# A transformer layer's first projection: the first two token tiles in halves by turns, smaller early loads, and one fold moved ahead

## The reference, cut to what matters

```
h = rmsnorm(x, p['norm_mix_g'])
z = h @ p['w_in']                    # x: tokens x 1024, w_in: 1024 x 2576
gq, gk, gv, gr, ga, pu, dq, dk, dv = jnp.split(z, idx, axis=-1)
```

## Time and profile before

| | us |
|---|---|
| median of 3 runs | 747.88 (747.49 to 748.06) |
| profiled execution, its own time | 748.39 |
| its span | 746.5 |
| PE busy in it | 684.6 (92%) |
| DVE, ACT, POOL busy | 521.9, 424.1, 142.3 |

### The profile page before, as it was taken

The page is one execution under the profiler, slowest core; times in us unless marked ns, Lnnn a source line. Parts: engine busy times, 40 slices in busy tenths (PEclk is TensorE's granted clock), DMA queues, the critical chain, the costliest instruction groups (busy, mean ns, idle before and its releaser), DMA issues.

```text
span 746.5 us, 9430 instructions
## 1 busy us (share of the span) xinstructions
PE 684.6 (92%) x3469; PEld 550.8 (74%) x3469; DVE 521.9 (70%) x697; ACT 424.1 (57%) x602; POOL 142.3 (19%) x160
## 2 busy tenths in 40 slices
PE   4999999998887998889999589999999999999992
PEld 3898887776655675668888568888888888878861
DVE  4436745565577656266456779888999999988883
ACT  5635642245453443163334528888888788777881
POOL 4102840011000101100000220222222222222134
PEclk9999999999899999899999669999999999999997
DMA  8623242303771000130045879999999999999863
GB/s 305 211 82 152 94 159 99 113 22 114 261 283 69 2 1 0 57 141 0 1 177 219 293 278 326 369 389 366 384 379 375 382 374 375 373 369 382 321 215 128
DMA packets 32867, 161.23 MB, mean 216 GB/s; under 512 B 6189, under 2 KB 6523, under 8 KB 18108
## 3 DMA queue, kind: packets, MB, share of 16 engines
q1 hardware_dynamic: 23392, 140.39, 49.6%
q0 software_dynamic: 5344, 10.27, 5.1%
q10 hardware_dynamic: 4092, 10.08, 3.7%
HBM read 149.59 MB, written 20.03 MB: 227 GB/s over the span
## 4 chain that ended last, share of the span: by engine, by line
PE 71%; DVE 16%; DMA 4%; ACT 4%; issue 3%; POOL 1%; SPq 1%; POOLq 0%; DVEq 0%; ACTq 0%
PE pj L2111 41%; PE scores L2111 13%; PE tr_v L2111 10%; DVE wl L1414 4%; PE tr_a L2119 2%; PE scores L2491 2%; PE tr_v L2119 2%; DMA acc_rows<-y,idx_sb 1%; DMA xs_next<-acc_rows,idx_sb 1%; DVE w_lo L1414 1%; PE tr_a L2520 1%; ACT prob L1133 1%; DMA xT_raw<-in_xT 1%; DVE tiny L1667 1%; DVE w_lo L1443 1%
## 5 line engine op out<-in xcount | busy, mean ns | idle before, releaser
L1414 DVE TENSOR_TENSOR wl<-moe_raw,wh 128x2048 fp32r<-128x2048 f32 x96 | 218.5, 2290 | 26.9 <-ACT wh L901 26.1
L901 ACT ACTIVATE wh<-moe_raw 128x2048 fp32r<-128x2048 f32 x96 | 182.3, 1919 | 37.7 <-PE scores L2111 12.3
L2111 PE MATMUL pj<-w_hi,xT_hi 128*128 128x512 f32 (+2 forms) x192 | 70.9, 369 | 9.5 <-DVE w_lo L1443 7.8
L747 POOL TENSOR_SCALAR rs<-stat 128x1 f32<-128x1 f32 (+4 forms) x31 | 11.1, 359 | 338.1 <-ACT sq_scr L913 181.0
L2111 PE MATMUL pj<-w_hi,xT_lo 128*128 128x512 f32 (+2 forms) x192 | 69.1, 360 | 0.0
L2111 PE MATMUL pj<-w_lo,xT_hi 128*128 128x512 f32 (+2 forms) x192 | 69.1, 360 | 0.0
L802 POOL DMA_INDIRECT acc_rows<-y,idx_sb x14 | 22.3, 1590 | 206.3 <-ACT y L1337 192.2
L2111 PE MATMUL pj<-wh,xgh 128*128 128x512 f32 x128 | 52.2, 408 | 1.4 <-DVE xgl L1414 1.4
L1443 DVE SCALAR_TENSOR_TENSOR w_lo<-raw,pack_a,w_hi 128x512 fp32r<-128x512 f32 (+2 forms) x64 | 43.8, 744 | 12.2 <-ACT w_hi L945 12.1
L2111 PE MATMUL tr_v<-wh,xgh 128*128 128x512 f32 x128 | 51.1, 399 | 0.0
L2111 PE MATMUL pj<-wh,xgl 128*128 128x512 f32 x128 | 50.5, 395 | 0.0
(11 more groups left out here) (416 smaller groups left out, 1500.6 us busy)
## 6 DMA issues: line engine op xcount, KB each, us to landing
moe_raw<-in_w_exp_gate SPq DMA_DIRECT2D x32, 1024.0 KB, 8.9
moe_raw<-in_w_exp_up SPq DMA_DIRECT2D x32, 1024.0 KB, 10.2
moe_raw<-in_w_exp_down SPq DMA_DIRECT2D x32, 1024.0 KB, 10.7
raw<-in_dense SPq DMA_DIRECT2D x16, 1024.0 KB, 5.9
raw<-in_dense SPq DMA_DIRECT2D x8, 256.0 KB, 6.9
x_rows<-in_x_prompt SPq DMA_DIRECT2D x4, 512.0 KB, 11.0
xw<-in_x_prompt ACTq DMA_DIRECT2D x1, 2048.0 KB, 8.5
h_rows<-h ACTq DMA_DIRECT2D x4, 512.0 KB, 3.6
```

Source lines behind the costliest of these rows:

```text
L747: link(pool.tensor_scalar(rs[rows, n, cs], stat[rows, n, cs], EPS, None, ALU.add))
L901: act.activation(wh[s4][:, :], moe_raw[n % RING][:, :], ACT.Copy).then_inc(hi_done, 1)
L1414: return dve.tensor_tensor(out, a, b, op)
L2111: return pe.matmul(out, lhsT, rhs, start=start, stop=stop, skip_group_check=True)
```

## The change

**Loads.** x tiles 0, 1 and 2 are loaded in halves (x_half), the first half of tile 1 ahead of the last quarter of unit 0; the second half of tile 1, both halves of tile 2 and tile 3 follow unit 1, and only then rows 0, rows 1, x tile 4, rows 2, unit 2, and so on. ACT's first load takes only 27 columns of pack_a; the other 316 are loaded by ACT after the high part of x tile 4, and DVE waits for them (pack_in) ahead of their first use.

**Products.** PE takes G tiles 0 and 1 half by half in turn: k 0 to 3 of tile 0, k 0 to 3 of tile 1, k 4 to 7 of tile 0, k 4 to 7 of tile 1. Tile 2 is taken in two halves as well. G tiles 2 and 3 go to the last two banks of `scores`, G tiles 0, 1 and 4 to pj0, pj1, pj0. The transposes come one tile later (tile t-3 ahead of tile t for t = 3, 4; tile 2 ahead of R tile 0; tiles 3 and 4 after R tiles 0 and 1).

**ACT and DVE.** High and low parts follow the new order of arrival; all of x tiles 1 to 3 stand ahead of squares 0 and 1. The split of unit 2 stands ahead of the copy of G tile 2 as before, that of unit 3 after it. On DVE the fold of the sample tile of G stands ahead of the copies of tile 3's transpose, where it stood ahead of tile 4's.

```diff
-    plan = [((b, t), row_reader(t)) for b, _, _ in IN_BLOCKS[:-1] for t in range(TILES)] + [(("Q", t), "A") for t in range(2)]
+    plan = [(("G", t), row_reader(t), (0, 1, 2, 3, 0)[t]) for t in range(TILES)]
+    plan += [((b, t), row_reader(t)) for b, _, _ in IN_BLOCKS[1:-1] for t in range(TILES)] + [(("Q", t), "A") for t in range(2)]
     for t in range(TILES):
...
         sc = ctx.enter_context(nc.psum_tensor("scores", [P, 4 * 512], F32))
+        pj_more = [sc[:, 1024:1536], sc[:, 1536:2048]]
+        pj_of = lambda key: (pj + pj_more)[PJ[key][3]]
...
         moe_in = [sem(f"moe_in{i}") for i in range(RING)]
-        x_in, x0_in = [sem(f"x_in{t}") for t in range(TILES)], [sem(f"x0_in{g}") for g in range(2)]
+        x_in, xh_in = {t: sem(f"x_in{t}") for t in (3, 4)}, [[sem(f"x{t}_in{g}") for g in range(2)] for t in range(3)]
         part_in = [[sem(f"unit{n}_in{k}") for k in range(4)] for n in range(2)]
...
         x_again = sem("x_again")
-        gains_in = sem("gains_in")
+        gains_in, pack_in = sem("gains_in"), sem("pack_in")
         mem_in, params_in, hist_in, state_in = sem("mem_in"), sem("params_in"), sem("hist_in"), sem("state_in")
...
-            for n in range(2):
-                ks = slice(4 * n, 4 * n + 4)
-                sp.dma_start(xT_raw[:, 0, ks, :], A["xT"][0][:, ks, :]).then_inc(x0_in[n], 16)
+            def x_half(t, g):
+                ks = slice(4 * g, 4 * g + 4)
+                sp.dma_start(xT_raw[:, t, ks, :], A["xT"][t][:, ks, :]).then_inc(xh_in[t][g], 16)
+
+            def quarter(n, k):
+                c = slice(512 * k, 512 * k + 512)
+                sp.dma_start(raw[:, n, c], unit(n)[:, c]).then_inc(part_in[n][k], 16)
+
+            for g in range(2):
+                x_half(0, g)
                 for k in range(4):
-                    c = slice(512 * k, 512 * k + 512)
-                    sp.dma_start(raw[:, n, c], unit(n)[:, c]).then_inc(part_in[n][k], 16)
-            for t in range(1, 4):
-                x_load(t)
-                rows_load(t - 1)
+                    quarter(g, k)
+                    if (g, k) == (0, 2):
+                        x_half(1, 0)
+            x_half(1, 1)
+            x_half(2, 0)
+            x_half(2, 1)
+            x_load(3)
+            rows_load(0)
+            rows_load(1)
+            x_load(4)
+            rows_load(2)
             dense_load(2)
-            x_load(4)
             rows_load(3)
...
-            act.dma_start(pack_a[:, :], A["pack_a"]).then_inc(gains_in, 16)
+            act.dma_start(pack_a[:, 0:27], A["pack_a"][:, 0:27]).then_inc(gains_in, 16)
...
-            def x0_high(g):
+            def x_half_high(t, g):
                 ks = slice(4 * g, 4 * g + 4)
-                act.wait_ge(x0_in[g], 16)
-                act.activation(xT_hi[:, 0, ks, :], xT_raw[:, 0, ks, :], ACT.Copy).then_inc(xT_hi_done, 1)
+                act.wait_ge(xh_in[t][g], 16)
+                act.activation(xT_hi[:, t, ks, :], xT_raw[:, t, ks, :], ACT.Copy).then_inc(xT_hi_done, 1)
...
-            x0_high(0)
+            x_half_high(0, 0)
             act.wait_ge(gains_in, 16)
             w_high(0)
-            x0_high(1)
+            x_half_high(1, 0)
+            x_half_high(0, 1)
             w_high(1)
+            x_half_high(1, 1)
+            for g in range(2):
+                x_half_high(2, g)
+            x_high(3)
             act.wait_ge(consts, 1)
             for t in range(2):
-                x_high(t + 1)
                 x_square(t)
+            x_high(4)
+            act.dma_start(pack_a[:, 27:], A["pack_a"][:, 27:]).then_inc(pack_in, 16)
             act.dma_start(pack_b[:, :], A["pack_b"]).then_inc(params_in, 16)
...
             for t in range(4):
-                if t >= 2:
-                    w_high(t)
+                if t == 2:
+                    w_high(2)
                 n = t
...
                 pj_out(("G", t), rowbuf[0:r, n % 2, 0:256], rs[0:r, 1, t:t + 1],
-                       pj[PJ[("G", t)][3]][0:r, 0:256]).then_inc(act_step, 1)
+                       pj_of(("G", t))[0:r, 0:256]).then_inc(act_step, 1)
                 steps[0] += 1
                 pj_out(("G", t), gv[0:r, t, :], rs[0:r, 1, t:t + 1],
-                       pj[PJ[("G", t)][3]][0:r, 256:512]).then_inc(pj_act, 1)
-                if t < 2:
-                    x_high(t + 3)
+                       pj_of(("G", t))[0:r, 256:512]).then_inc(pj_act, 1)
+                if t == 2:
+                    w_high(3)
                 if t < 3:
...
-            def x0_low(g):
+            def x_half_low(t, g, n):
                 ks = slice(4 * g, 4 * g + 4)
-                dve.wait_ge(xT_hi_done, g + 1)
-                tt(xT_lo[:, 0, ks, :], xT_raw[:, 0, ks, :], xT_hi[:, 0, ks, :].bitcast(F32), ALU.subtract).then_inc(xT_lo_done, 1)
+                dve.wait_ge(xT_hi_done, n)
+                tt(xT_lo[:, t, ks, :], xT_raw[:, t, ks, :], xT_hi[:, t, ks, :].bitcast(F32), ALU.subtract).then_inc(xT_lo_done, 1)
             def x_low(t):
-                dve.wait_ge(xT_hi_done, t + 2)
+                dve.wait_ge(xT_hi_done, t + 4)
                 if t < 4:
...
             link(dve.memset(lg[:, :, :], 0.0))
-            for n in range(2):
-                x0_low(n)
-                w_low(n)
-            for t in range(1, TILES):
-                x_low(t)
+            x_half_low(0, 0, 1)
+            w_low(0)
+            x_half_low(1, 0, 2)
+            x_half_low(0, 1, 3)
+            w_low(1)
+            x_half_low(1, 1, 4)
+            for g in range(2):
+                x_half_low(2, g, 5 + g)
+            x_low(3)
+            x_low(4)
...
             for t in range(TILES):
-                if t in (2, 3):
-                    w_low(t)
-                if t == 4:
+                if t in (1, 2):
+                    w_low(t + 1)
+                if t == 3:
                     n = ROW_AT[("G", 4)]
...
             dve.tensor_reduce(lams[:, 1:2], lamv[:, 2, :], AX.X, ALU.add).then_inc(lam_sum, 1)
+            dve.wait_ge(pack_in, 16)
             link(dve.tensor_scalar(gdiff[:, :], gdiff[:, :], 1.0 - LAM_INIT, None, ALU.mult))
...
                     claim("pj", PJ, PJ_KEYS, key, pj_act, pj_dve)
-                out = pj[j][:, 0:w]
+                out = pj_of(key)[:, 0:w]
                 for k in range(nk) if part is None else range(part * nk // 2, (part + 1) * nk // 2):
                     n, c = units[k // 4], slice(w * (k % 4), w * (k % 4) + w)
-                    if key == ("G", 0) and k == 4:
-                        pe.wait_ge(xT_lo_done, 2)
                     if t == 0:
...
                 for t in range(TILES):
-                    pe.wait_ge(xT_lo_done, t + 2 if t else 1)
                     project((b, t), t, *x_block(t), BLOCK_UNITS[b], WIDTH[b])
...
-            in_block("G", 2, {})
-            in_block("R", 0, {0: lambda: rows_T("G", 4, 2)})
+            for part in range(2):
+                for t in range(2):
+                    pe.wait_ge(xT_lo_done, 2 * part + t + 1)
+                    project(("G", t), t, *x_block(t), BLOCK_UNITS["G"], WIDTH["G"], part)
+            for part in range(2):
+                pe.wait_ge(xT_lo_done, 5 + part)
+                project(("G", 2), 2, *x_block(2), BLOCK_UNITS["G"], WIDTH["G"], part)
+            for t in range(3, TILES):
+                rows_T("G", t - 3, 2)
+                pe.wait_ge(xT_lo_done, t + 4)
+                project(("G", t), t, *x_block(t), BLOCK_UNITS["G"], WIDTH["G"])
+            rows_T("G", 2, 2)
+            in_block("R", 0, {0: lambda: rows_T("G", 3, 2), 1: lambda: rows_T("G", 4, 2)})
             in_block("U", 2, {0: gate_T, 1: gate_logits})
...
```

## The result

The first comparison gave 740.87 us median (739.99 to 742.88, 4 runs) against 747.88 (747.49 to 748.06), a ratio of 0.9907 [0.9888, 0.9927]: 7.0 us less, below the forecast range. It did not hold at that size. The same two kernels compared twice more gave 743.39 against 746.55, 0.9949 [0.9922, 0.9976], and 743.18 against 747.96, 0.9941 [0.9914, 0.9967]. Over all executions that are listed with their mean granted clock (the share of 2.4 GHz that the matmul clock had over the execution), the kernel before has a mean of 746.92 us (133 runs, 742.05 to 752.61, standard error 0.20) and the changed one 742.73 (26 runs, 739.83 to 746.83, error 0.43). So the change takes off **4.2 us (error 0.5)**, 0.56%, or 3.9 without the four executions of the first comparison; the forecast was 2.2.

What follows compares the result with a forecast made beforehand. PE, busy 92% of the span, was taken as the bound, with time to win where it waits or runs slowly. Gains of 1.96 and 0.3 us, rounded to 2.2, took 747.88 to 745.7, range 744.6 to 747.5.

Steps and rivals of the forecast that it cites:

- The hole: Block G, between tiles 0 and 1: PE waits for x tile 1, 2.08 us from start to start; predicted to go.
- 36.3 (2.2 before 38.5): Sign in the trace after: block R's first matmul near 36.3 us, 2.2 us sooner than before.
- the sum of 2.26: Whole forecast gain, 1.96 us from the turns plus 0.3 from the smaller first load, rounded to 2.2.
- Together 1.96: Turns in block G: 1.85 us of waiting for x tile 1 and 0.11 of a slow first step saved.
- I take 0.3: Smaller first load of pack_a, at PE's start and unit 0's fourth quarter: 0.3 us gain, from 0 to 0.5.
- the rise of the clock I let move with PE's start: Block G: the step from 1.2 to 2.4 GHz, 4.8 us after PE's first matmul, assumed to shift with that matmul.
- the runs' scatter of 0.3: Whole-kernel time: run-to-run scatter of 0.3 us, used in setting the range's lower end at 744.6.
- Rival 1: Clock rises later in block G (1.8 us lost, 747.5) or has another half low stretch at 188-200 us (1.7); chance 0.17.
- The parts priced at nothing: G tiles 2 and 3 in `scores` banks, later transposes, and the moved fold: each priced at 0 us.
- hold PE about 2 us: Ahead of R tile 1: the fold behind the copy of tile 3's transpose would end 2.5 us later, delaying PE.
- Rival 2: Gains come late: pack_a's small piece takes 5.8 us instead of 3.6, delaying unit 0's first quarter; some 746.8, chance 0.08.
- Rival 4: Slower: rows 0 land after about 23.0 us, PE stands at the transpose ahead of G tile 3; chance 0.05.

Runs made afterwards that it cites:

- the warm ones: The changed kernel with 36 or 30 needless bf16 matmuls of 128x128 ahead of PE's first real one: 742.27 and 742.29 us in the mean.
- the 13 matmuls: 13 needless 128x512 matmuls between blocks G and R, in the kernel before and in the changed one: 748.75 and 747.61 us in the mean.
- a_steady: The changed kernel with 14 or 6 needless bf16 matmuls in each differential attention step from the third on: 743.20 us in the mean.
- b_steady: The kernel before with 14 or 6 needless bf16 matmuls in each differential attention step from the third on: 746.61 us in the mean.
- b_warm: The kernel before with 36 needless bf16 matmuls of 128x128 ahead of PE's first real one: median 746.45 us, ratio 0.9983.
- a_fold_back: The changed kernel with the fold of G's sample tile put back to tile 4 on DVE: 748.51 us, ratio 1.0016.

## Why the prediction was wrong

**The mechanism was right.** The hole is gone in all four profiles of the changed kernel: after its first matmul PE waits for nothing in block G. G tile 2 came at 20.27 to 21.70 (20.8 was said), R at 35.41 to 36.84 (36.3), R tile 1 waited for nothing. The mean of R's start is 38.3 in the four profiles of before (38.51, 38.22, 37.71, 38.78) and 36.1 in the four of after, 2.2 us sooner. That this is the forecast's number is partly luck. One transpose fewer (0.22 us) stands ahead of R now, which "36.3 (2.2 before 38.5)" left out; the sum of 2.26 should have shown as some 2.5 there. At block U's start, with equal work behind, the means are 52.95 and 50.96: **2.0 us**.

**The two terms.** "Together 1.96" for the turns: with them but the whole pack_a, block U starts at 51.18 in one profile, 1.8 before the kernel before's, and the runs are 2.0 ± 0.5 less at equal clock. "I take 0.3" for the smaller first load: PE's first matmul came no sooner (7.81 in the mean, before 7.85; 7.3 to 7.8 was said). The changed kernel's block U is 0.2 sooner in the mean than that of the one profile with the whole pack_a, and the runs say 0.7 ± 0.6, so the term is neither confirmed nor refuted. What the prediction did not see is that the small load alone closes most of the same hole: in the kernel before the bytes also stood ahead of x tile 1, for which PE waited. It came 1.3 us sooner in the mean, where 0.56 was reckoned by bytes, and block U started at 51.70 and 51.74, 1.2 sooner. Alone the two are worth 1.2 and 1.8, together 2.0. Splitting and reordering the loads without the turns adds nothing to the small load (block U at 51.92).

**Rise of the clock.** "the rise of the clock I let move with PE's start" was too simple: it came between 11.2 and 13.9 us with PE's start between 7.67 and 7.97. Before, R followed x tile 1 (split at 14.30, 14.88, 15.17 and 15.42, R at 37.71, 38.22, 38.51 and 38.78), and the hole swallowed a late rise. After, nothing does: rises at 11.2, 11.5, 13.0 and 13.9 put R at 35.41, 35.77, 36.31 and 36.84.

**The step that failed by most was "the runs' scatter of 0.3".** It took three runs within 0.6 us for the scatter of the kernel, and so closed the range at 744.6. The kernel before goes from 742.05 to 752.61. Of the 7.0 us of the first comparison, 2.8 are draws of that kind: the median of before was 1.0 above its long mean, that of after 1.9 below its own. Rival 1 had the right price, 1.7 us for 3.4 us at 1.2 GHz, but counted only a loss; the stretches go both ways.

**The other 4.2 us** are 2.7 ± 0.3 at equal clock, against the 2.0 of block U's start, and 1.5 by the mean clock, 0.9673 against 0.9648. The cut between the two isn't sharp: 3.4 us at 1.2 GHz are worth 1.7 us and 0.0023 of the mean clock, so 0.001 should go with 0.74 us and not with the line's 0.59, and by that the shares would be 2.3 and 1.9. The profiles leave little room for a third share. The span less block U's start less half of all time at 1.2 GHz is 664.6 us in the four profiles of before (663.1 to 666.3) and 664.1 in the four of after (663.7 to 664.4). So the first projection gives 2.0 us, and most of the rest is time at 1.2 GHz.

Why the changed kernel is granted more in the mean stays open. That a wait in the first 45 us is answered 170 us later is one candidate: the kernels in which PE waits there had 0.9639 to 0.9659, the small load alone (0.5 us of waiting) among them. But the warm ones wait too (steps of 1.1 and 2.0 us) and had 0.9667 and 0.9680. That the middle stages lie at another place in time is the other candidate, and the 13 matmuls speak for it. No run separated the two. Nor is it shown that the clock is all: with a mean clock of 0.973 for both, a_steady and b_steady were still 3.4 ± 0.6 us apart, though block U started only 1.8 sooner in their profiles. With errors near 0.001 of clock in the small samples this can't be settled.

**The parts priced at nothing** cost nothing. The banks and the later transposes show no wait. The fold, "hold PE about 2 us" at the wrong place, held it 2.65, and a low stretch behind it cost 1.7 more. Rival 2 did not happen: the 13.5 KB piece landed 3.0 us after its issue, and the first quarter was split at 6.02. The Trainium skill, "DMA: Bandwidth & Descriptors", Specifications, says that below 512 bytes the engine reads, modifies and writes, which speaks against its rows of 108 bytes. No run here shows a cost from it. Rival 4 did not either: G tile 0's copy ended at 22.3, 3.4 us before PE wanted it, where 1.3 to 3 were said.

## What to carry to other kernels

Put ahead in the queues only what the first products need: 158 KB that could wait cost more than their bytes at the arrival that PE waited for, and moving them alone gave 1.2 us where the whole change gave 2.0 at block U. Compare two orders where equal work lies behind both, not at a landmark that the change itself moved. When two edits close the same hole, their prices don't add; price the second with the first in place. And before a forecast within 1% is believed or a result is read, take some twenty runs with their granted clocks: here 0.001 of mean clock was 0.6 us, and the first four runs overstated the effect by 2.8 us.

## What the runs showed of the hardware

- Time at 1.2 GHz in the middle of the kernel came in stretches of 3.4 us, two to five of them, at places that vary from execution to execution of the same kernel. With them a single core's time scatters by 1.4% (742.05 to 752.61 us).
- Between 200 and 320 us the plain kernels' eight profiles have one to three such stretches; with needless matmuls in the waits of that stage both kernels had one, and a mean clock of 0.973 in place of 0.965 and 0.967.
- 36 bf16 matmuls of 128x128 on constants, 3.7 us of them, had the clock at its higher level for the first real matmul (a step of 0.30 us at 8.12, then 0.23), where without them it rose at 10.4 to 14.4 us in the other profiles.
- In b_warm a hole of 2.24 us from start to start was followed by 3.4 us at 1.2 GHz, from about 1.3 us after PE resumed, and in a_fold_back one of 3.03 us (2.65 of waiting) by as much, from 0.4 us after. Holes of 1.9 to 2.2 us in six other profiles were not followed by any. b_warm had two more holes ahead of its own (steps of 0.94 us from 10.05 and 1.10 from 11.55), where the six had at most one (0.90 in b_steady). What decides was not tested.
- A load of 171.5 KB in rows of 1372 bytes on another queue in place of one of 13.5 KB had x tile 1 split 1.3 us later in the mean (four profiles against two), where the 158 KB more are 0.56 us at the 287 GB/s of the earlier trace rows.
